# MLP up projections with weight tiles as the stationary operand, activations and their remainder side by side as the moving operand

## The chip, the cores and the metric

The program runs on one core of a Trainium2 chip. The metric is the device time of one execution in microseconds (us). The kernel before takes 2648.08 us, the median of three runs.

## The reference

Two transformer blocks in float32 on 256 tokens of 2048 features: a block with a pooling mixer and dilated attention, then one with a gated delta rule, a convolution and cross attention to a memory. Both end in the MLP that this change touches:

```python
h = rmsnorm(x, norm_mlp_g[l])
x = x + jnp.square(jax.nn.relu(h @ w_up[l])) @ w_down[l]      # w_up 2048 x 8192, w_down 8192 x 2048
```

The second block has the same with `mlp_w1_2`, `mlp_w2_2`.

## The kernel before, in words

Every large product is a sum of three: each float32 number is split into a high part and a remainder, both held as fp32r, and hi·hi, hi·remainder and remainder·hi are accumulated in PSUM. Weights come from HBM in *steps* of 1 MB (128 partitions x 2048 numbers); they are never reused.

- SyncE issues one DMA per step into one of five slots `weights_raw` (`load`), once the step five back is used up (`w_used`).
- ScalarE copies a step to `weights_hi` (three slots, L1249), two steps ahead of TensorE at most; VectorE writes the remainder `weights_lo` over the raw slot (L1691).
- TensorE multiplies (`step`, L677, L678, L681): a step holds two k-tiles of 128 rows by 1024 columns of weights. For each of two token tiles and two k-tiles a 128x128 tile of activations is stationary and 512 weight columns move: 24 matmuls of 128x512 a step. Eight steps are a *pass*: 1024 output columns, in one of two groups of four PSUM banks.

The activations stand transposed as `stationary_hi` and `stationary_lo` (features on partitions), which the steps read. They are made by TensorE transposes and a split on ScalarE and VectorE.

In `mlp` a half of the 8192 hidden features takes four up passes and then two down passes of 16 steps each; there are two halves and two MLPs, so 16 up passes and 8 down passes. An up pass leaves tokens on partitions, while the down passes want hidden features on partitions. So after each up pass ScalarE takes relu with the scale `rstd` (`relu`, L1300), VectorE multiplies by the positive part (`square`, L1743), TensorE turns the result with 16 transposes (`turn_hidden`, L729, placed two steps into the next pass), and ScalarE and VectorE split it into `hidden_hi` (L1307) and `hidden_lo` (L1751). For the MLP norm `rstd` holds one over the mean square, and the scale stands on the hidden rows once.

Each engine runs its instructions in program order. ScalarE and VectorE loop over steps k: `split_next(s0 + k)` splits step k+1, and after it comes what belongs to that point of the pass.

Of the kernel before, what the change touches and what calls it, by code (L numbers as in the profile page):

```python
# [7 lines left out]
F32 = mybir.dt.float32  # L8
F32R = mybir.dt.float32r
# [4 lines left out]
P = 128  # L14
# [14 lines left out]
AHEAD = 1  # L29

# [60 lines left out]
def build(nc, x, mem, vectors, squares, alibi, pool_avg, w_in, pool_w, pool_scale, w_out, w_up, w_down,  # L91
          final_g, w_in2, a_log, dt_bias, w_out2, wq, wk, wv, wo, w1, w2, final_g2, out):
    ctx = ExitStack()
    with ctx:
# [12 lines left out]
        HHI = at("stationary_hi", [P, KT, T], 16, F32R)  # L107
        HLO = at("stationary_lo", [P, KT, T], 32, F32R)
# [29 lines left out]
        JUNK = at("squares_unused", [P, TT, D], A0 + 64)  # L138
        AHI = at("hidden_hi", [P, HK, T], A0 + 0, F32R)
        ALO = at("hidden_lo", [P, HK, T], A0 + 32, F32R)  # L140
        R = at("hidden", [P, TT, COLS], A0 + 64)
# [140 lines left out]
        relu_done = sem("relu_done")  # L282
        r_turned = sem("r_turned")
# [122 lines left out]
        HALF_PASSES = 6  # L406
# [45 lines left out]
        def blocks(w):  # L452
            return w.rearrange("(s j p) n -> s p j n", j=STEP, p=P)
# [5 lines left out]
        def _(sp):  # L459
# [165 lines left out]
        def _(pe):  # L625
# [90 lines left out]

            def mlp(m, s_m, p_m, h, while_last=None):
                pe.wait_ge(ht_lo, KT * h + KT // 2)
                for half in range(2):
                    s0, p0, a0 = s_m + half * HALF_STEPS, p_m + half * HALF_PASSES, 32 * m + 16 * half  # L720
# [12 lines left out]
                    for p in range(4):  # L733
                        if p >= 2:

                            pe.wait_ge(at_hi, a0 + 4 * (p - 1))
                            pe.wait_ge(at_lo, a0 + 4 * (p - 1))
                        for k in range(PS):
                            if p >= 1 and k == 2:
                                turn_hidden(p - 1)  # L740
                            if p == 0 and half == 0:
                                if k == 2:

                                    left(p0 - 1)
                                    turn8(residual, 1, 1)
                                stationary(h, STEP * (k + 1))
                            step(s0 + p * PS + k, HHI, HLO, STEP * k, p0 + p, k == 0, k == PS - 1)
                    for d in range(2):
                        n = HK // STEP
                        pe.wait_ge(at_hi, a0 + 12 + 4 * d)  # L750
                        pe.wait_ge(at_lo, a0 + 12 + 4 * d)
                        for k in range(n):
                            if d == 0 and k == 2:
                                turn_hidden(3)
                            if d == 0 and k == 12:
                                pe.wait_ge(at_hi, a0 + 16)
                                pe.wait_ge(at_lo, a0 + 16)
                            if while_last and half and d and k == 4:
                                while_last()
                            step(s0 + 4 * PS + d * n + k, AHI, ALO, STEP * k, p0 + 4 + d, k == 0, k == n - 1)  # L760
# [477 lines left out]
        def _(act):  # L1238
# [47 lines left out]
            def mlp(m, s_m, p_m, norm, h, g_of):  # L1286
                for half in range(2):
                    s0, p0, r0 = s_m + half * HALF_STEPS, p_m + half * HALF_PASSES, 32 * m + 16 * half
# [983 lines left out]
```

## Time and profile before

| what | value |
|---|---|
| median, lowest, highest of three runs | 2648.08, 2645.53, 2648.35 us |
| span of the profiled execution, first to last instruction | 2644.1 us |
| TensorE: matmul busy, weight loads busy | 2623.9 us (99%), 2190.3 us (83%) |
| VectorE, ScalarE busy | 1448.3 us (55%), 1106.6 us (42%) |
| matmuls | 12420 |
| mean DMA rate | 178 GB/s |

The time of the profiled execution as a whole is not recorded apart from its span; the median of the runs is 4.0 us above that span. "Busy" of TensorE is not a rate: matmuls overlap in the records (a 128x512 one is shown with 390 ns), so how long each costs is read from the distance between starts, or from the chain of waits, which gives each its own share of the time.

### The profile page before, as it was taken

What the parts mean: (1) busy time and instruction counts of PE and PEld (TensorE: products, weight loads), DVE (VectorE), ACT (ScalarE), POOL (GpSimd) and SP (SyncE); (2) the same over time, 40 slices, a digit from 0 to 9 for tenths busy, and PEclk for the clock granted to TensorE, in tenths of its full rate; (3) what the DMA queues carried; (4) which work ended last, traced back from release to release, by engine and by line L of the source; (5) the groups of instructions that cost most, each with busy time, mean ns of one, the idle gap of its engine ahead of it and who ended that gap; (6) DMA issues with size and microseconds to landing.
All of it is one profiled execution on the core that took longest, in us unless ns stands there. A gap on an engine that the chain in (4) does not pass through costs nothing.

```text
span 2644.1 us, 28753 instructions
## 1 busy us (share of the span) xinstructions
PE 2623.9 (99%) x12420; PEld 2190.3 (83%) x12420; DVE 1448.3 (55%) x1249; ACT 1106.6 (42%) x966; POOL 40.7 (2%) x58
## 2 busy tenths in 40 slices
PE   9999999999999999999999999999999999999998
PEld 7888888888888888888888888887888888888887
DVE  5464545544455445677658796544554544455444
ACT  5344444433344334454225444443454433344433
POOL 0000000000000000001000000000000000000000
PEclk9999999999999999999999999999999999999999
DMA  8544655566555566655324355553555566555564
GB/s 292 198 147 143 206 185 185 187 191 191 193 189 184 186 188 190 233 181 161 111 82 142 121 187 185 176 160 127 175 207 177 190 191 191 192 190 181 187 194 138
DMA packets 121980, 471.56 MB, mean 178 GB/s; under 512 B 7328, under 2 KB 7968, under 8 KB 120704
## 3 DMA queue, kind: packets, MB, share of 16 engines
q1 hardware_dynamic: 119440, 456.62, 53.2%
q0 software_dynamic: 1856, 11.54, 1.2%
q8 instruction: 99, 1.62, 0.2%
q10 hardware_dynamic: 560, 1.57, 0.2%
q14 instruction: 25, 0.20, 0.0%
HBM read 465.51 MB, written 4.19 MB: 178 GB/s over the span
## 4 chain that ended last, share of the span: by engine, by line
PE 96%; DVE 3%; ACT 1%; issue 0%; DMA 0%; POOLq 0%; SPq 0%; POOL 0%; ACTq 0%; DVEq 0%
PE ps L677 29%; PE ps L678 29%; PE ps L681 29%; PE ps L913 2%; DVE conv_out L1903 1%; PE ps L729 1%; PE ps L641 1%; PE ps L799 1%; DVE weights_lo L1691 1%; PE ps L1165 1%; PE ps L1181 1%; PE ps L1085 0%; PE ps L1087 0%; PE ps L1010 0%; PE ps L880 0%; PE ps L871 0%
## 5 line engine op out<-in xcount | busy, mean ns | idle before, releaser
L1691 DVE TENSOR_TENSOR weights_lo<-weights_raw,weights_hi 128x2048 fp32r<-128x2048 f32 x431 | 987.6, 2292 | 958.6 <-ACT weights_hi L1249 958.6
L1249 ACT ACTIVATE weights_hi<-weights_raw 128x2048 fp32r<-128x2048 f32 x431 | 826.4, 1918 | 1165.4 <-PE ps L681 1164.1
L677 PE MATMUL ps<-weights_hi,stationary_hi 128*128 128x512 f32 x2432 | 960.2, 395 | 6.5 <-ACT stationary_hi L1592 2.5
L678 PE MATMUL ps<-weights_lo,stationary_hi 128*128 128x512 f32 x2432 | 949.9, 391 | 0.0
L681 PE MATMUL ps<-weights_hi,stationary_lo 128*128 128x512 f32 x2432 | 750.9, 390 | 0.0
L677 PEld LDWEIGHTS ps<-weights_hi,stationary_hi 128*128 128x128 f32 x2432 | 457.5, 188 | 103.1 <-issue 5.2
L681 PEld LDWEIGHTS ps<-weights_hi,stationary_lo 128*128 128x128 f32 x2432 | 457.7, 188 | 96.3
L678 PEld LDWEIGHTS ps<-weights_lo,stationary_hi 128*128 128x128 f32 x2432 | 458.2, 188 | 92.4 <-issue 0.7
L677 PE MATMUL ps<-weights_hi,hidden_hi 128*128 128x512 f32 x1016 | 396.0, 390 | 0.0
L678 PE MATMUL ps<-weights_lo,hidden_hi 128*128 128x512 f32 x1016 | 395.8, 390 | 0.0
L681 PE MATMUL ps<-weights_hi,hidden_lo 128*128 128x512 f32 x1016 | 312.9, 389 | 0.0
L677 PEld LDWEIGHTS ps<-weights_hi,hidden_hi 128*128 128x128 f32 x1016 | 190.8, 188 | 39.4
L681 PEld LDWEIGHTS ps<-weights_hi,hidden_lo 128*128 128x128 f32 x1016 | 190.8, 188 | 39.4
L678 PEld LDWEIGHTS ps<-weights_lo,hidden_hi 128*128 128x128 f32 x1016 | 190.9, 188 | 39.2
L1903 DVE SCALAR_TENSOR_TENSOR conv_out<-conv_in,vectors,conv_out 128x256 f32<-128x256 f32 x240 | 100.8, 500 | 0.2
L1267 ACT ACTIVATE stationary_hi<-ps,vectors 128x256 fp32r<-128x256 f32 x120 | 45.5, 488 | 50.7 <-PE ps L641 50.7
L1704 DVE SCALAR_TENSOR_TENSOR stationary_lo<-ps,vectors,stationary_hi 128x256 fp32r<-128x256 f32 x120 | 48.5, 477 | 21.7 <-ACT stationary_hi L1267 21.7
L1307 ACT ACTIVATE hidden_hi<-ps 128x512 fp32r<-128x512 f32 x64 | 33.1, 604 | 62.5 <-PE ps L729 62.5
L1751 DVE TENSOR_TENSOR hidden_lo<-ps,hidden_hi 128x512 fp32r<-128x512 f32 x64 | 39.8, 685 | 35.4 <-ACT hidden_hi L1307 35.4
L1300 ACT ACTIVATE hidden<-ps,rstd 128x1024 f32<-128x1024 f32 x32 | 35.7, 1117 | 37.6 <-PE ps L681 37.6
L1743 DVE SCALAR_TENSOR_TENSOR hidden<-ps,hidden 128x1024 f32<-128x1024 f32 x32 | 39.1, 1222 | 18.5 <-ACT hidden L1300 18.5
L1724 DVE TENSOR_TENSOR residual<-ps,residual 128x1024 f32<-128x1024 f32 x26 | 31.8, 1222 | 0.1
(312 smaller groups left out, 1011.0 us busy)
## 6 DMA issues: line engine op xcount, KB each, us to landing
weights_raw<-in_w SPq DMA_DIRECT2D x128, 1024.0 KB, 5.2
weights_raw<-in_w_in SPq DMA_DIRECT2D x79, 1024.0 KB, 5.1
weights_raw<-in_w_up SPq DMA_DIRECT2D x64, 1024.0 KB, 4.8
weights_raw<-in_w_down SPq DMA_DIRECT2D x64, 1024.0 KB, 5.5
weights_raw<-in_w_out SPq DMA_DIRECT2D x32, 1024.0 KB, 5.4
weights_raw<-in_wk SPq DMA_DIRECT2D x16, 1024.0 KB, 5.3
weights_raw<-in_wv SPq DMA_DIRECT2D x16, 1024.0 KB, 5.3
weights_raw<-in_wq SPq DMA_DIRECT2D x16, 1024.0 KB, 5.3
```

The source lines that it names most:

```text
L677: pe.matmul(o, xh, WHI[:, slot, j, c * BANK:(c + 1) * BANK], start=first and j == 0, stop=False)
L678: pe.matmul(o, xh, WLO[:, low, j, c * BANK:(c + 1) * BANK], start=False, stop=False)
L681: mm = pe.matmul(o, xl, WHI[:, slot, j, c * BANK:(c + 1) * BANK], start=False, stop=last and j == STEP - 1)
L913: last = pe.matmul(ps[:, 4 + u // 4, (u % 4) * P:(u % 4 + 1) * P], lhs[:, u, :], rhs[:, u, :], start=True, stop=True)
L1249: act.activation(WHI[:, s % NSPLIT], RAW[:, s % NRAW], ACT.Copy).then_inc(hi_ready, 1)
L1267: act.activation(HHI[:, k, :], v, ACT.Copy, scale=gain(g(k))).then_inc(ht_hi, 1)
L1300: act.activation(R[:, t, :], ps[:, g + 2 * t:g + 2 * t + 2, :].rearrange("p b n -> p (b n)"), ACT.Relu, scale=rstd_of(norm, t)).then_inc(r ...
L1691: dve.tensor_tensor(WLO[:, s % NRAW], RAW[:, s % NRAW], WHI[:, s % NSPLIT].bitcast(F32), ALU.subtract).then_inc(lo_ready, 1)
L1704: dve.scalar_tensor_tensor(HLO[:, k, :], v, gain(g(k)), HHI[:, k, :].bitcast(F32), ALU.mult, ALU.subtract).then_inc(ht_lo, 1)
L1743: dve.scalar_tensor_tensor(R[:, t, :], ps[:, g + 2 * t:g + 2 * t + 2, :].rearrange("p b n -> p (b n)"), 0.0, R[:, t, :], ALU.max, ALU.mult ...
L1751: dve.tensor_tensor(ALO[:, k:k + 2, :].rearrange("p k t -> p (k t)"), ps[:, g + b, :], AHI[:, k:k + 2, :].bitcast(F32).rearrange("p k t -> ...
L1903: last = dve.scalar_tensor_tensor(COUT31[:, c, :], src, dw_tap(j, c), COUT31[:, c, :], ALU.mult, ALU.add)
```

## The change

In the up passes a 128x128 tile of weights is stationary (128 of the columns of `w_up`) and the activations move. High part and remainder of a k-tile's activations now lie side by side (`HX`), so one matmul of 128x512 with the high weights gives both hi·hi (256 columns) and hi·remainder (the other 256), and one of 128x256 with the low weights adds remainder·hi to the first 256. The output has features on partitions and tokens on the free axis, as the down passes want it, and `turn_hidden` is gone. The two sums in a bank are added by ScalarE (copy of the second part) and VectorE (add, then relu times value). An up pass is 512 features in four steps of four k-tiles; there are 32 of them. `rstd` moves behind the down products (`add_scaled`, and the last additions). Rows of `w_up` are loaded in pieces of 512 columns rather than 1024.

```diff
+UPS = 4
+UPT = BANK // P
...
-        HHI = at("stationary_hi", [P, KT, T], 16, F32R)
-        HLO = at("stationary_lo", [P, KT, T], 32, F32R)
+        HX = at("stationary", [P, KT, 2, T], 16, F32R)
+        HHI, HLO = HX[:, :, 0, :], HX[:, :, 1, :]
...
-        R = at("hidden", [P, TT, COLS], A0 + 64)
+        UB = at("up_second_part", [P, UPT, T], A0 + 64)
+        UZ = at("up", [P, UPT, T], A0 + 68)
...
+            def load_up(s, src):
+                if s >= NRAW:
+                    sp.wait_ge(w_used, s - NRAW + 1)
+                dst = RAW[:, s % NRAW].rearrange("p j (h c) -> p (j h) c", c=BANK)
+                sp.dma_start(dst, src).then_inc(raw_landed[s % NRAW], 16)
...
-                    for p in range(4):
-                        c0 = half * HALF + p * COLS
-                        for k in range(PS):
-                            load(h0 + p * PS + k, blocks(up)[k, :, :, c0:c0 + COLS])
+                    for p in range(UP_PASSES):
+                        c0 = half * HALF + p * BANK
+                        for k in range(UPS):
+                            load_up(h0 + p * UPS + k, blocks(up, KT // UPS)[k, :, :, c0:c0 + BANK])
...
+            def up_tile(slot, low, q, c, k, group, start, stop):
+                col = (q % 2) * BANK + c * P
+                o = ps[:, 4 * group + c, :]
+                pe.matmul(o, WHI[:, slot, q // 2, col:col + P], HX[:, k, :, :].rearrange("p a t -> p (a t)"), start=start, stop=False)
+                return pe.matmul(o[:, 0:T], WLO[:, low, q // 2, col:col + P], HX[:, k, 0, :], start=False, stop=stop)
+
+            def up_step(s, k, p, arriving=None):
+
+                pe.wait_ge(hi_ready, s + 1)
+                pe.wait_ge(lo_ready, s + 1)
+                slot, low, group = s % NSPLIT, s % NRAW, GROUPS[p]
+                before = [n for n in range(p) if GROUPS[n] == group]
+                nq = KT // UPS
+                if k < UPS - 1:
+                    for q in range(nq):
+                        if arriving is not None:
+                            stationary(arriving, nq * k + q + 1)
+                        for c in range(UPT):
+                            if k == 0 and q == 0 and c % 2 == 0:
+                                pe.wait_ge((out0, out1)[c // 2], before[-1] + 1)
+                            mm = up_tile(slot, low, q, c, nq * k + q, group, k == 0 and q == 0, False)
+                else:
+                    for c in range(UPT):
+                        for q in range(nq):
+                            if arriving is not None and c == 0:
+                                stationary(arriving, nq * k + q + 1)
+                            mm = up_tile(slot, low, q, c, nq * k + q, group, False, q == nq - 1)
+                        if c == 1:
+                            mm.then_inc(t0_done, 1)
+                mm.then_inc(w_used, 1)
...
-                    def turn_hidden(p):
-                        pe.wait_ge(out0, p0 + p + 1)
-                        pe.wait_ge(out1, p0 + p + 1)
-                        g = 4 * (p % 2)
-                        for b in range(4):
-                            for k in range(2 * b, 2 * b + 2):
-                                for t in range(TT):
-                                    last = pe.transpose(ps[:, g + b, (k % 2) * T + t * P:(k % 2) * T + (t + 1) * P],
-                                                        R[:, t, k * P:(k + 1) * P], IDENT)
-                            last.then_inc(r_turned, 1)
...
+                    for p in range(UP_PASSES):
+                        for k in range(UPS):
+                            if (half, p, k) == (0, 0, 1):
+
+                                left(p0 - 1)
+                                turn8(residual, 1, 1)
+                            up_step(s0 + p * UPS + k, k, p0 + p, h if (half, p) == (0, 0) else None)
...
-                    def relu(p):
-                        act.wait_ge(rstd_ready, norm + 1)
-                        if p >= 1:
-                            act.wait_ge(r_turned, r0 + 4 * p)
-                        g = 4 * (p % 2)
-                        for t in range(TT):
-                            if t == 0:
+                    s0, p0 = s_m + half * HALF_STEPS, p_m + half * HALF_PASSES
+                    a0 = 2 * UP_PASSES * m + UP_PASSES * half
+
+                    def second_part(p):
+                        g = 4 * GROUPS[p0 + p]
+                        for n in range(2):
+                            if n == 0:
                                 act.wait_ge(t0_done, p0 + p + 1)
                             else:
-                                act.wait_ge(w_used, s0 + (p + 1) * PS)
-                            act.activation(R[:, t, :], ps[:, g + 2 * t:g + 2 * t + 2, :].rearrange("p b n -> p (b n)"), ACT.Relu,
-                                           scale=rstd_of(norm, t)).then_inc(relu_done, 1)
+                                act.wait_ge(w_used, s0 + (p + 1) * UPS)
+                            if p >= 1:
+                                act.wait_ge((out0, out1)[n], p0 + p)
+                            act.activation(UB[:, 2 * n:2 * n + 2, :], ps[:, g + 2 * n:g + 2 * n + 2, T:2 * T], ACT.Copy).then_inc(up_moved, 1)
 
                     def hidden_hi(p):
-                        g = 4 * (p % 2)
-                        for b in range(4):
-                            act.wait_ge(r_turned, r0 + 4 * p + b + 1)
-                            act.activation(AHI[:, 8 * p + 2 * b:8 * p + 2 * b + 2, :].rearrange("p k t -> p (k t)"), ps[:, g + b, :], ACT.Copy).then_inc(at_hi, 1)
+                        act.wait_ge(up_squared, a0 + p + 1)
+                        act.activation(AHI[:, UPT * p:UPT * p + UPT, :], UZ[:], ACT.Copy).then_inc(at_hi, 1)
...
+            def add_scaled(s_end, p, c0, norm):
...
+                    dve.scalar_tensor_tensor(v, ps[:, g:g + 2, :].rearrange("p b n -> p (b n)"), rstd_of(norm, t), v, ALU.mult, ALU.add).then_inc(o, 1)
...
-                    def square(p):
-                        g = 4 * (p % 2)
-                        for t, o in enumerate((out0, out1)):
-                            dve.wait_ge(relu_done, h0 + 2 * p + t + 1)
-                            dve.scalar_tensor_tensor(R[:, t, :], ps[:, g + 2 * t:g + 2 * t + 2, :].rearrange("p b n -> p (b n)"), 0.0, R[:, t, :],
-                                                     ALU.max, ALU.mult).then_inc(o, 1)
+                    s0, p0 = s_m + half * HALF_STEPS, p_m + half * HALF_PASSES
+                    a0 = 2 * UP_PASSES * m + UP_PASSES * half
+
+                    def squared(p):
+                        g = 4 * GROUPS[p0 + p]
+                        for n, o in enumerate((out0, out1)):
+                            dve.wait_ge(up_moved, 2 * (a0 + p) + n + 1)
+                            dve.tensor_tensor(UZ[:, 2 * n:2 * n + 2, :], ps[:, g + 2 * n:g + 2 * n + 2, 0:T], UB[:, 2 * n:2 * n + 2, :], ALU.add).then_inc(o, 1)
+                        dve.wait_ge(out1, p0 + p + 1)
+                        dve.scalar_tensor_tensor(UZ[:], UZ[:], 0.0, UZ[:], ALU.max, ALU.mult).then_inc(up_squared, 1)
 
                     def hidden_lo(p):
-                        g = 4 * (p % 2)
-                        for b in range(4):
-                            dve.wait_ge(at_hi, a0 + 4 * p + b + 1)
-                            k = 8 * p + 2 * b
-                            dve.tensor_tensor(ALO[:, k:k + 2, :].rearrange("p k t -> p (k t)"), ps[:, g + b, :],
-                                              AHI[:, k:k + 2, :].bitcast(F32).rearrange("p k t -> p (k t)"), ALU.subtract).then_inc(at_lo, 1)
+                        dve.wait_ge(at_hi, a0 + p + 1)
+                        dve.tensor_tensor(ALO[:, UPT * p:UPT * p + UPT, :], UZ[:], AHI[:, UPT * p:UPT * p + UPT, :].bitcast(F32), ALU.subtract).then_inc(at_lo, 1)
...
```

How TensorE's order changes. Before, at the third step of the second up pass of the first MLP: the end of a step, then the transposes of the pass before (`squares` is the identity, `hidden` the squared relu).

```order
L681 MATMUL ps<-weights_hi,stationary_lo 128x512 x2
L729 MATMUL ps<-squares,hidden 128x128 [waits out1,out0]
L729 MATMUL ps<-squares,hidden 128x128 x15
L677 MATMUL ps<-weights_hi,stationary_hi 128x512 [waits lo_ready,hi_ready]
L678 MATMUL ps<-weights_lo,stationary_hi 128x512
```

Of the changed kernel, where the third up pass of the first MLP begins; `stationary` is now the moving operand and `weights_hi`, `weights_lo` are the stationary one:

```order
L731 MATMUL ps<-stationary,weights_hi 128x512
L732 MATMUL ps<-stationary,weights_lo 128x256
L731 MATMUL ps<-stationary,weights_hi 128x512 [waits out0,lo_ready,hi_ready]
L732 MATMUL ps<-stationary,weights_lo 128x256
L731 MATMUL ps<-stationary,weights_hi 128x512
L732 MATMUL ps<-stationary,weights_lo 128x256
L731 MATMUL ps<-stationary,weights_hi 128x512 [waits out1]
```

A step is now 16 pairs of a 128x512 and a 128x256 matmul, with a new weight tile for each of the two, and no transposes stand between steps.

ScalarE before, at the end of the first up pass (`t0_done`: first half of the pass's last step, `w_used`: the step's end):

```order
L1249 ACTIVATE weights_hi<-weights_raw 128x2048 [waits w_used,raw_landed2]
L1300 ACTIVATE hidden<-ps,rstd 128x1024 [waits t0_done,rstd_ready]
L1300 ACTIVATE hidden<-ps,rstd 128x1024 [waits w_used]
L1249 ACTIVATE weights_hi<-weights_raw 128x2048 [waits w_used,raw_landed3]
L1249 ACTIVATE weights_hi<-weights_raw 128x2048 [waits w_used,raw_landed4]
L1307 ACTIVATE hidden_hi<-ps 128x512 [waits r_turned] x4
```

and of the changed kernel:

```order
L1270 ACTIVATE weights_hi<-weights_raw 128x2048 [waits w_used,raw_landed3]
L1321 ACTIVATE up_second_part<-ps 128x512 [waits t0_done]
L1321 ACTIVATE up_second_part<-ps 128x512 [waits w_used]
L1270 ACTIVATE weights_hi<-weights_raw 128x2048 [waits w_used,raw_landed4]
L1325 ACTIVATE hidden_hi<-up 128x1024 [waits up_squared]
```

The split of the hidden features follows one step after the pass's end rather than two, and comes after every fourth step, not every eighth.

## Rows read from the trace of the kernel before

**Rows 1.** The page: the chain that ended last, by engine and by line.
```profile
PE 96%; DVE 3%; ACT 1%; issue 0%; DMA 0%; POOLq 0%; SPq 0%; POOL 0%; ACTq 0%; DVEq 0%
```
**Rows 2.** Windows: up passes, then down passes; us, busy (instructions), PEclk, DMA share, GB/s.
```profile
314.00:495.60 181.60, 181.60 (x836) 151.36 (x835) 93.33 (x60) 81.69 (x64) 1.49 (x3) 1.00 0.56 191
495.50:680.00 184.50, 184.50 (x824) 153.07 (x823) 85.73 (x43) 67.68 (x39) 0.00 (x0) 1.00 0.61 193
```
**Rows 3.** The chain in order of time, up passes: start us, us, what.
```profile
355.92 0.45 PE ps L681 x2
...
361.36 0.45 PE ps L681 x2
...
369.98 1.75 PE ps L729 x16
...
415.29 1.75 PE ps L729 x16
```
**Rows 4.** The chain from the beta and alpha product (L926 to L928) on.
```profile
1062.36 0.12 PE ps L926
...
1067.98 0.23 PE ps L677
```
**Rows 5.** Timeline, loads alone, same place: start us, us, engine, line, what.
```profile
1062.20 0.10 PEld L927 LDWEIGHTS ps<-stationary_hi,w_ba_lo 128*16 128x16 f32 x1
1062.32 0.09 PEld L928 LDWEIGHTS ps<-stationary_lo,w_ba_hi 128*16 128x16 f32 x1
```
**Rows 6.** Timeline at L1110 (matmuls of two columns): matmuls, then loads.
```profile
1621.44 3.63 PE L1110 MATMUL ps<-squares,conv_squares 128*128 128x2 f32 x32
```
```profile
1621.21 3.77 PEld L1110 LDWEIGHTS ps<-squares,conv_squares 128*128 128x128 f32 x32
```
**Rows 7.** Groups by form: weight loads, count, busy us, mean ns of one.
```profile
L678 PEld LDWEIGHTS ps<-weights_lo,stationary_hi 128*128 128x128 f32 x2432 | 458.2, 188 | 92.4 <-issue 0.7
L913 PEld LDWEIGHTS ps<-inverse_t,level_product 128*128 128x128 f32 x160 | 18.5, 192 | 0.5
```
**Rows 8.** The chain: matmuls of 128x128 and of 128x256 in plain float32.
```profile
1289.56 3.57 PE ps L913 x32
...
1771.16 6.91 PE ps L1165 x32
```
**Rows 9.** Timeline of loads and matmuls in an up pass.
```profile
345.33 0.19 PEld L678 LDWEIGHTS ps<-weights_lo,stationary_hi 128*128 128x128 f32 x1
345.56 0.19 PEld L677 LDWEIGHTS ps<-weights_hi,stationary_hi 128*128 128x128 f32 x1
```
```profile
345.33 0.39 PE L677 MATMUL ps<-weights_hi,stationary_hi 128*128 128x512 f32 x1
345.55 0.39 PE L678 MATMUL ps<-weights_lo,stationary_hi 128*128 128x512 f32 x1
```
**Rows 10.** The page's groups, ScalarE and VectorE: busy us, mean ns of one.
```profile
L1307 ACT ACTIVATE hidden_hi<-ps 128x512 fp32r<-128x512 f32 x64 | 33.1, 604 | 62.5 <-PE ps L729 62.5
L1751 DVE TENSOR_TENSOR hidden_lo<-ps,hidden_hi 128x512 fp32r<-128x512 f32 x64 | 39.8, 685 | 35.4 <-ACT hidden_hi L1307 35.4
L1300 ACT ACTIVATE hidden<-ps,rstd 128x1024 f32<-128x1024 f32 x32 | 35.7, 1117 | 37.6 <-PE ps L681 37.6
L1743 DVE SCALAR_TENSOR_TENSOR hidden<-ps,hidden 128x1024 f32<-128x1024 f32 x32 | 39.1, 1222 | 18.5 <-ACT hidden L1300 18.5
L1724 DVE TENSOR_TENSOR residual<-ps,residual 128x1024 f32<-128x1024 f32 x26 | 31.8, 1222 | 0.1
```
**Rows 11.** Timeline of ScalarE at a pass's end: in brackets the idle time before.
```profile
359.13 1.12 ACT L1300 ACTIVATE hidden<-ps,rstd 128x1024 f32<-128x1024 f32 x1 [1.54 <-PE ps L681]
360.14 1.91 ACT L1249 ACTIVATE weights_hi<-weights_raw 128x2048 fp32r<-128x2048 f32 x1
364.63 1.92 ACT L1249 ACTIVATE weights_hi<-weights_raw 128x2048 fp32r<-128x2048 f32 x1 [2.58 <-PE ps L681]
```
**Rows 12.** DMA queues in 0 to 30 us, then in 314 to 495 us: packets, MB, share of 16 engines.
```profile
q10 hardware_dynamic: 272, 0.52, 5.4%
```
```profile
q1 hardware_dynamic: 8704, 33.56, 54.9%
...
weights_raw<-in_w_up SPq DMA_DIRECT2D x28, 1024.0 KB, 4.8
```

More of the change, by code:

```diff
@@ L281, in build @@
         ht_lo = sem("ht_lo")
[L282 to L283 removed]
+        up_moved = sem("up_moved")
+        up_squared = sem("up_squared")
         at_hi = sem("at_hi")
@@ L733, in mlp @@
[L733 to L747, printed above, removed]
+                    s0, p0, a0 = s_m + half * HALF_STEPS, p_m + half * HALF_PASSES, 2 * UP_PASSES * m + UP_PASSES * half
@@ L752, in mlp @@
                         for k in range(n):
[L753 to L757, printed above, removed]
+                            if d == 0 and k == n - 2:
+                                pe.wait_ge(at_hi, a0 + UP_PASSES)
+                                pe.wait_ge(at_lo, a0 + UP_PASSES)
@@ L758, in mlp @@
                             if while_last and half and d and k == 4:
                                 while_last()
-                            step(s0 + 4 * PS + d * n + k, AHI, ALO, STEP * k, p0 + 4 + d, k == 0, k == n - 1)
+                            step(s0 + UP_PASSES * UPS + d * n + k, AHI, ALO, STEP * k, p0 + UP_PASSES + d, k == 0, k == n - 1)
             def keep_busy(n):
@@ L1309, in mlp @@
                     for k in range(AHEAD, HALF_STEPS + AHEAD):
                         split_next(s0 + k)
-                        p = k // PS - 1
-                        if 0 <= p < 4 and k % PS == 0:
-                            relu(p)
-                        elif 0 <= p < 4 and k % PS == 2:
-                            hidden_hi(p)
+                        if UPS <= k < UPS * (UP_PASSES + 1) and k % UPS == 0:
+                            second_part(k // UPS - 1)
+                        elif UPS <= k < UPS * (UP_PASSES + 1) and k % UPS == 1:
+                            hidden_hi(k // UPS - 1)
@@ L1316, in mlp @@
                         elif half == 0 and k == 1:
+                            split_turned(h, lambda k: g_of + k, 1, 1)
+                        elif half == 0 and k == 3:
                             act.wait_ge(out1, p_m)
-                            squares_of(X, norm)
-                        elif half == 0 and k == 2:
-                            split_turned(h, lambda k: g_of + k, 1, 1)
+                            squares_of(X, norm, MLP_JUNK)
                         elif m == 0 and half == 1 and k == HALF_STEPS - HK // STEP + 4:
@@ L1728, in ahead @@
                     split_next(s0 + k)
+            def add_scaled(s_end, p, c0, norm):
+                dve.wait_ge(rstd_ready, norm + 1)
+                for t, o in enumerate((out0, out1)):
+                    if t == 0:
+                        dve.wait_ge(t0_done, p + 1)
+                    else:
+                        dve.wait_ge(w_used, s_end)
+                    g = 4 * GROUPS[p] + 2 * t
+                    v = X[:, t, c0:c0 + COLS]
+                    dve.scalar_tensor_tensor(v, ps[:, g:g + 2, :].rearrange("p b n -> p (b n)"), rstd_of(norm, t), v, ALU.mult, ALU.add).then_inc(o, 1)
             def ahead_and_residual(s_next, p):
@@ L1754, in mlp @@
+                    def hidden_lo(p):
+                        dve.wait_ge(at_hi, a0 + p + 1)
+                        dve.tensor_tensor(ALO[:, UPT * p:UPT * p + UPT, :], UZ[:], AHI[:, UPT * p:UPT * p + UPT, :].bitcast(F32), ALU.subtract).then_inc(at_lo, 1)
                     for k in range(AHEAD, HALF_STEPS + AHEAD):
                         split_next(s0 + k)
-                        p = k // PS - 1
-                        if 0 <= p < 4 and k % PS == 0:
-                            square(p)
-                        elif 0 <= p < 4 and k % PS == 2:
-                            hidden_lo(p)
-                        elif half == 0 and k == 2:
+                        if UPS <= k < UPS * (UP_PASSES + 1) and k % UPS == 0:
+                            squared(k // UPS - 1)
+                        elif UPS <= k < UPS * (UP_PASSES + 1) and k % UPS == 1:
+                            hidden_lo(k // UPS - 1)
+                        elif half == 0 and k == 1:
@@ L1762, in mlp @@
                             split_turned(h, lambda k: g_of + k, 1, 1)
                         elif k == HALF_STEPS // 2 + HK // STEP:
-                            add_residual(s0 + k, p0 + 4, 0)
+                            add_scaled(s0 + k, p0 + UP_PASSES, 0, norm)
                         elif m == 0 and half == 1 and k == HALF_STEPS - HK // STEP + 4:
@@ L1772, in mlp @@
                         elif k == HALF_STEPS and (m, half) != (1, 1):
-                            add_residual(s0 + k, p0 + 5, COLS)
+                            add_scaled(s0 + k, p0 + UP_PASSES + 1, COLS, norm)
             dve.memset(ZEROS[:], 0.0).then_inc(zeros_ready, 1)
```

26 lines of the change are left out of this document (13 added, 13 removed).

## The prediction

> **What bounds the kernel now.** First the chain of waits: 96% of the span runs through TensorE [rows 1]. Then the windows of one half of an MLP: in its up passes TensorE is busy for all of 181.60 us, while VectorE has 93 us of work, ScalarE 82 and the DMA engines a share of 0.56, at the full granted clock [rows 2]. Nothing waits there that could be shortened; only TensorE's own instructions count. Their durations must not be read from the groups (390 ns for a 128x512 matmul), since they overlap. In the chain the same place of a step recurs after 5.44 us (355.92 to 361.36) [rows 3]; a step has 24 matmuls, so one costs 226.7 ns. The 16 transposes after an up pass stand in the chain with 1.75 us [rows 3], 109 ns each. Pass to pass is 415.29 - 369.98 = 45.31 us, which is 8 x 5.44 + 1.75 = 45.27: the up stage is these two terms and nothing else.
>
> **What goes.** 16 up passes with 16 transposes each: 16 x 1.75 = 28.0 us. The matmuls: 16 passes x 8 steps x 24 = 3072 at 226.7 ns, 696.4 us. Together 724.4 us.
>
> **What comes.** 32 passes x 4 steps x 16 = 2048 pairs: a 128x512 matmul and a 128x256 one. The columns that move are the same as before (3072 x 512 = 2048 x 768), but there are 4096 matmuls for 3072, each with a weight tile of its own, and half of them are short. So the case is decided by what a short fp32r matmul costs when the next 128x128 tile has to be loaded under it.
>
> The long one: 226.7 ns, unchanged; its successor's load begins as it begins (the load for L678 at 345.33, where the matmul of L677 starts; the next at 345.56 beside 345.55 [rows 9]) and has time enough.
>
> The short one: the trace has 48 fp32r matmuls of 256 columns in a row, 1062.36 to 1067.98 us in the chain [rows 4], which is 117.1 ns each. But their weight tiles have only 16 columns (0.09 us a load [rows 5]); with 128 columns this pairing doesn't occur. What a load of 128 columns costs when nothing covers it shows where matmuls have two columns: 32 loads take 3.77 us, so (3.77 - 0.19)/31 = 115 ns with one delay among them, and 32 matmuls in 3.63 us, (3.63 - 0.25)/31 = 109 [rows 6]. Matmuls of 128 columns in plain float32 with new weights each come to 3.57/32 = 112 ns [rows 8]. So a load needs 109 to 115 ns, though its record says 188 or 192 [rows 7]; the records overlap, as the spacing of 112 at a duration of 192 shows. Those loads are of plain float32; the fp32r ones have the same record (188), and I take the same spacing. The load of 109 to 115 just fits under a matmul of 117.1. Bounds for the short one: from below 109 (the load alone); from above 188, the whole record of a load laid bare, and beyond it 6.91/32 = 216 ns, the 128x256 matmul in plain float32 [rows 8], another type of operand. I take 118, next to the row of the same type and length, with 1 ns for a load that is as good as tight.
>
> The up stage after: 2048 x (226.7 + 118) ns = 705.9 us. Against 724.4 that is -18.5 us: the matmuls cost 9.5 us more, the transposes give 28.0 back. Each nanosecond of the short matmul is 2.05 us of the sum, and the gain is gone at 118 + 18.5/2.05 = 127 ns.
>
> A rule of the Trainium skill speaks against this. "TensorE: Matmul & The Clock Gate", section "Packing small matmuls", says that a load of weights runs beside matmuls in flight only where it goes to other rows of the array. Here all loads fill all rows and yet run beside [rows 9], so the trace disagrees. By the rule the 1024 additional pairs would lay bare a load each, by the 112 ns of the rows 115 us, and the change would end near 2744 us.
>
> **What is hidden.** ScalarE and VectorE. With E the end of an up pass on TensorE: ScalarE copies the second half of the second part (128x512 from PSUM, 604 ns by L1307), VectorE adds it (685 by L1751) and multiplies (128x1024, 1222 by L1743) [rows 10]; done near E + 2.7. Then ScalarE has put the split of the step after next in between (1.9 us), and writes `hidden_hi` (1117 by L1300), done near E + 3.9; VectorE follows with the low weights (2.29 us, from about E + 2.8) and then `hidden_lo` (1222), done near E + 6.4. Behind these waiting instructions the splits of weights are queued, for which TensorE waits. But the split after the pass's end is for the step that starts at E + 11: before too ScalarE splits it right behind its work for the pass (360.14) and the next one only when TensorE is a step further (364.63, after 2.58 us idle) [rows 11]. There are some 5 us in hand. By pass of 22 us VectorE has 4 x 2.29 + 2 x 0.685 + 2 x 1.222 = 13.0 us and ScalarE 4 x 1.92 + 2 x 0.604 + 1.117 = 10.0. The hidden features of pass 7 are wanted 14 steps later, and the bank group of a pass a whole pass later. Zero from both; if the cover failed, each pass start would show it, 32 times.
>
> `add_scaled` in place of the plain addition: both forms take 1222 ns from PSUM [rows 10], and the last two pairs of additions, which are on the chain, change alike: zero. The transposes of the residual at the start of each MLP move one step forward; two of these, and the steps behind them need the result one and a half steps later: zero. Ends of both signs within 1 us.
>
> The loads: rows of 2 KB in place of 4 KB for `w_up`, 512 packets a step. In the up passes a packet of 4 KB takes 0.549 x 16 x 181 us / 8704 = 183 ns; the queue that brought a part of x in pieces of 2 KB took 0.054 x 16 x 30 us / 272 = 95 ns a packet [rows 12]. So a step needs 512 x 95/16 = 3.0 us of all engines against 256 x 183/16 = 2.9, in 5.5 us. SyncE's queue may issue a step's load two steps before ScalarE wants it, 11 us against 4.8 to landing [rows 12]. Zero; a packet of 2 KB would have to cost 172 ns before it decides.
>
> **Sum.** Span 2644.1 - 18.5 = 2625.6 us; the median of the runs is 4.0 above this span, so 2629.6 us.
>
> **The rivals.**
> 1. *The short matmul doesn't cover its load* (the side of slower). Place: each of the 2048 second loads and swaps. For it: the records of 188 ns, loads at 83% of the span, and that the pairing isn't in the trace; also that a 128x512 fp32r matmul already costs 13 ns more than 512 columns at 2.4 GHz (213.3), and I don't know from what. Against it: the rows at 109 to 115. It decides from 127 ns: at 135 it is +16 us (2664), at 188 it is 2048 x 70 ns = 143 us over the forecast (2773), at 216 it is 2830. Chance 0.11, the milder half of it likelier.
> 2. *A new wait at pass boundaries*: ScalarE's and VectorE's tail, 0.3 us at each of 32 starts gives back 10 us: 2640. For it: twice as many boundaries; against it: 5 us in hand. Chance 0.05.
> 3. *The loads in 2 KB rows decide*: if a packet of 2 KB cost as much as one of 4 KB (183 ns), a step would take 5.86 us and 128 steps 44 us more: 2673. Against it 95 ns. Chance 0.02.
> 4. *A larger gain*: the load alone sets the short matmul, 109 ns: another 18 us, 2611. For it: half of 226.7 is 113. Against it the 48 at 117.1. Chance 0.07. The Trainium skill, same page, section "Back-to-back issue gap", gives N/2.4 + 2.5 ns, 109 for 256 columns; by that the sum would also be 2611, but it gives 216 for 512 columns, where the rows have 226.7.
> 5. The forecast, short matmul 115 to 122: 0.75; by itself 2623 to 2638.
>
> **Range and chances.** Rivals 2 and 4 in large part and the first edge of rival 1 belong in the range: 2618 to 2646. What can be told from no change here is about 0.2%, 5.3 us, so faster means under 2642.8: the forecast, rivals 4 and 2 (most) and a little of 1, 0.86. Within 0.2% (to 2653, short matmul 124 to 130): 0.06. Slower 0.08.
>
> **What would show it.** In the chain of the up passes: L731 with 0.23 and L732 with 0.12 us, a step of 5.52 us, a pass of 22.1, no L729, a half's up stage at 176.5 us. Matmuls 12420 - 3072 - 256 + 4096 = 13188. ScalarE's and VectorE's splits still preceded by idle time that TensorE ends. Wrong if L732 stands at 0.13 or more, if the starts of steps have idle time on TensorE released by `weights_lo` or a DMA, or if the distance of a 128x512 matmul changes from 226.7 ns when activations move and weights stand.

## The result, and the profile after

The changed kernel takes 2639.67 us, the median of 11 runs (2638.12 to 2641.41), the kernel before 2647.82 (11 runs). The ratio is 0.9976, 95% interval [0.9967, 0.9984]: a gain of 0.24%, or 6.4 us. The two medians are 8.2 us apart, and the span of the profiled execution fell by 6.0, from 2644.1 to 2638.1 us. By any of the three the gain is a third to under a half of the 18.5 us forecast.

The page after, busy time and instructions, then the chain by engine (against [rows 1]):

```profile
PE 2617.4 (99%) x13188; PEld 2211.5 (84%) x13188; DVE 1485.3 (56%) x1281; ACT 1110.3 (42%) x966; POOL 40.6 (2%) x58
...
PE 96%; DVE 3%; ACT 1%; issue 0%; DMA 0%; POOLq 0%; SPq 0%; POOL 0%; ACTq 0%; DVEq 0%
```

13188 matmuls as counted; still TensorE alone. Windows over the up passes of a first half and of the second half behind it; columns as in [rows 2]:

```profile
314.80:493.00 178.20, 178.20 (x1035) 155.95 (x1034) 102.85 (x70) 83.56 (x66) 1.49 (x3) 1.00 0.61 194
668.90:849.50 180.60, 180.60 (x1024) 156.69 (x1023) 99.75 (x62) 76.76 (x55) 0.00 (x0) 1.00 0.58 187
```

The windows do not end exactly with the stages, which the starts of the matmuls give: 314.81 to 494.15 us is 179.3 us for the first half's 8 x 64 pairs with 16 transposes of the residual (1.75 us) among them, 668.25 to 849.14 is 180.9 us for the second half's with none. Before, the first half's columns and four sets of 16 transposes (three of the hidden rows, one of the residual) took 181.6. TensorE is busy throughout, at the full granted clock. So the difference between the two halves is neither waits nor clock, but the matmuls themselves: their distance must be read. Timeline of TensorE in a first half, then in a second (start us, us, engine, line):

```profile
345.08 0.39 PE L731 MATMUL ps<-stationary,weights_hi 128*128 128x512 f32 x1
345.31 0.27 PE L732 MATMUL ps<-stationary,weights_lo 128*128 128x256 f32 x1
345.42 0.40 PE L731 MATMUL ps<-stationary,weights_hi 128*128 128x512 f32 x1
345.65 0.28 PE L732 MATMUL ps<-stationary,weights_lo 128*128 128x256 f32 x1
...
346.12 0.40 PE L731 MATMUL ps<-stationary,weights_hi 128*128 128x512 f32 x1
```

```profile
669.30 0.40 PE L731 MATMUL ps<-stationary,weights_hi 128*128 128x512 f32 x1
...
670.00 0.40 PE L731 MATMUL ps<-stationary,weights_hi 128*128 128x512 f32 x1
670.24 0.28 PE L732 MATMUL ps<-stationary,weights_lo 128*128 128x256 f32 x1
670.36 0.40 PE L731 MATMUL ps<-stationary,weights_hi 128*128 128x512 f32 x1
```

Three pairs take 346.12 - 345.08 = 1.04 us in the first half and 670.36 - 669.30 = 1.06 us in the second. A pass has 346.7 ns a pair in the first halves of both MLPs and 353.3 in the second halves (distance of the long matmuls' starts, mean over a pass). The forecast had 344.7. Read to the nanosecond, the distances repeat without change. I call such a repeating pattern a *raster*, and there are three:

| raster | where | long to long, ns | long to short, short to long (means) |
|---|---|---|---|
| A | first half of the first MLP | 343, 350 in turn: 346.7 | 231.7, 115.0 |
| B | first half of the second MLP | 346 or 347 always: 346.7 | 230.0, 116.7 |
| C | both second halves | 349, 350, 361 in turn: 353.3 | 236.7, 116.7 |

So the distance behind the long matmul is 3 to 10 ns above its 226.7 in all of them, and the one behind the short matmul is at or below the 118 of the forecast. The weight loads, in the same stretch as the first fence:

```profile
345.31 0.19 PEld L731 LDWEIGHTS ps<-stationary,weights_hi 128*128 128x128 f32 x1
345.43 0.19 PEld L732 LDWEIGHTS ps<-stationary,weights_lo 128*128 128x128 f32 x1
```

Each still begins with the matmul ahead of it, as in [rows 9], the one under the short matmul too: it is covered.

The other engines at a pass's end (339.0 us; ScalarE, then VectorE; idle time before in brackets), against [rows 11]:

```profile
339.53 1.91 ACT L1270 ACTIVATE weights_hi<-weights_raw 128x2048 fp32r<-128x2048 f32 x1
341.65 1.06 ACT L1325 ACTIVATE hidden_hi<-up 128x1024 fp32r<-128x1024 f32 x1 [0.21 <-DVE up L1774]
344.64 1.92 ACT L1270 ACTIVATE weights_hi<-weights_raw 128x2048 fp32r<-128x2048 f32 x1 [1.93 <-PE ps L732]
```

```profile
339.67 0.69 DVE L1772 TENSOR_TENSOR up<-ps,up_second_part 128x512 f32<-128x512 f32 x1 [1.23 <-ACT up_second_part L1321]
340.40 1.23 DVE L1774 SCALAR_TENSOR_TENSOR up<-up 128x1024 f32<-128x1024 f32 x1
341.54 2.29 DVE L1708 TENSOR_TENSOR weights_lo<-weights_raw,weights_hi 128x2048 fp32r<-128x2048 f32 x1
343.74 1.22 DVE L1778 TENSOR_TENSOR hidden_lo<-up,hidden_hi 128x1024 fp32r<-128x1024 f32 x1
```

`hidden_lo` ends at 345.0, 6 us after the pass; the next split still finds ScalarE idle until TensorE frees a slot. As forecast. The loads of `w_up` take 5.2 us to land instead of 4.8, and nobody waits for them:

```profile
weights_raw<-in_w_up SPq DMA_DIRECT2D x64, 1024.0 KB, 5.2
```

TensorE's waits differ in one place, the first up step of the second MLP: L731 waits 0.18 us at its first matmul and 0.20 at its third for the addition of the residual, where L677 before waited 0.2 once. The third bank is now wanted two pairs after the first rather than half a step later.

### The profile page after: what moved, and what is told of

It reads as the page before. It is cut to its first block, busy times and chain, and to the rows that moved or that the text cites. A ratio compares the mean times of both kernels' runs of the same rounds, so it can differ in the third digit from the quotient of the medians.

```text
span 2638.1 us, 30356 instructions
## 1 busy us (share of the span) xinstructions
PE 2617.4 (99%) x13188; PEld 2211.5 (84%) x13188; DVE 1485.3 (56%) x1281; ACT 1110.3 (42%) x966; POOL 40.6 (2%) x58
## 4 chain that ended last, share of the span: by engine, by line
PE 96%; DVE 3%; ACT 1%; issue 0%; DMA 0%; POOLq 0%; SPq 0%; POOL 0%; ACTq 0%; DVEq 0%
PE ps L688 20%; PE ps L692 20%; PE ps L689 20%; PE ps L731 18%; PE ps L732 9%; PE ps L934 2%; DVE conv_out L1928 1%; PE ps L652 1%; PE ps L820 1%; DVE weights_lo L1708 1%; PE ps L1186 1%; PE ps L1202 1%; PE ps L1106 0%; PE ps L1108 0%; PE ps L1031 0%; PE ps L901 0%
## 5 line engine op out<-in xcount | busy, mean ns | idle before, releaser
L731 PE MATMUL ps<-stationary,weights_hi 128*128 128x512 f32 x2048 | 717.6, 396 | 0.4 <-DVE residual L1741 0.4
L732 PE MATMUL ps<-stationary,weights_lo 128*128 128x256 f32 x2048 | 572.9, 280 | 0.0
L688 PE MATMUL ps<-weights_hi,stationary 128*128 128x512 f32 x1408 | 559.4, 397 | 6.2 <-ACT stationary L1609 2.5
L689 PE MATMUL ps<-weights_lo,stationary 128*128 128x512 f32 x1408 | 549.5, 390 | 0.0
L731 PEld LDWEIGHTS ps<-stationary,weights_hi 128*128 128x128 f32 x2048 | 384.2, 188 | 92.2 <-issue 0.6
L692 PE MATMUL ps<-weights_hi,stationary 128*128 128x512 f32 x1408 | 435.3, 390 | 0.0
L732 PEld LDWEIGHTS ps<-stationary,weights_lo 128*128 128x128 f32 x2048 | 386.3, 189 | 0.1
L688 PEld LDWEIGHTS ps<-weights_hi,stationary 128*128 128x128 f32 x1408 | 265.2, 188 | 63.5 <-issue 4.5
L692 PEld LDWEIGHTS ps<-weights_hi,stationary 128*128 128x128 f32 x1408 | 264.9, 188 | 56.2
L689 PEld LDWEIGHTS ps<-weights_lo,stationary 128*128 128x128 f32 x1408 | 265.3, 188 | 53.4 <-issue 0.7
L1288 ACT ACTIVATE stationary<-ps,vectors 128x256 fp32r<-128x256 f32 x120 | 45.6, 489 | 54.4 <-PE ps L652 54.4
L1772 DVE TENSOR_TENSOR up<-ps,up_second_part 128x512 f32<-128x512 f32 x64 | 44.0, 688 | 42.4 <-ACT up_second_part L1321 42.4
```

The source lines that it names most:

```text
L688: pe.matmul(o, xh, WHI[:, slot, j, c * BANK:(c + 1) * BANK], start=first and j == 0, stop=False)
L689: pe.matmul(o, xh, WLO[:, low, j, c * BANK:(c + 1) * BANK], start=False, stop=False)
L692: mm = pe.matmul(o, xl, WHI[:, slot, j, c * BANK:(c + 1) * BANK], start=False, stop=last and j == STEP - 1)
L731: pe.matmul(o, WHI[:, slot, q // 2, col:col + P], HX[:, k, :, :].rearrange("p a t -> p (a t)"), start=start, stop=False)
L732: return pe.matmul(o[:, 0:T], WLO[:, low, q // 2, col:col + P], HX[:, k, 0, :], start=False, stop=stop)
L1288: act.activation(HHI[:, k, :], v, ACT.Copy, scale=gain(g(k))).then_inc(ht_hi, 1)
```

## The experiments

**Which term is off?** Four kernels, measured together.

First the transposes alone, in the kernel before:

```diff
                                 for t in range(TT):
-                                    last = pe.transpose(ps[:, g + b, (k % 2) * T + t * P:(k % 2) * T + (t + 1) * P],
-                                                        R[:, t, k * P:(k + 1) * P], IDENT)
+                                    if (k % 2, t) == (0, 0):
+                                        last = pe.transpose(ps[:, g + b, (k % 2) * T + t * P:(k % 2) * T + (t + 1) * P],
+                                                            R[:, t, k * P:(k + 1) * P], IDENT)
```

> The kernel before with 4 instead of 16 transposes after each up pass (one for each bank; three quarters of the hidden features are left unturned, so the sums are not the reference's). Theory A (the transposes stand on TensorE's path with their full 109 ns): 16 x 12 x 109.4 ns = 21.0 us less, 2627 us. Theory B (something else would be late without them, so removing them gives less): 5 to 15 us less, and idle time of TensorE at L677 behind L729.

Measured 2626.08 us (5 runs), ratio to before 0.9922 [0.9909, 0.9934]; the span falls by 20.2 us to 2623.9. The chain at such a place, against the 1.75 us of [rows 3]:

```profile
370.64 0.44 PE ps L730 x4
```

Theory A came true: twelve transposes are worth what the chain gives them. The term of 28.0 us stands, and the missing gain is in the matmuls.

Then the second matmul of each pair on all 512 columns:

```diff
-                return pe.matmul(o[:, 0:T], WLO[:, low, q // 2, col:col + P], HX[:, k, 0, :], start=False, stop=stop)
+                return pe.matmul(o, WLO[:, low, q // 2, col:col + P], HX[:, k, :, :].rearrange("p a t -> p (a t)"), start=False, stop=stop)
```

> The changed kernel with the second matmul of a pair on all 512 columns too (it adds low weights times remainder, a fourth product that the kernel leaves away). No matmul is short then. Theory A (only the mix of lengths costs extra): a pair is 2 x 226.7 = 453.3 ns, against 350.4 now, +103 ns x 2048 = +211 us, 2851 us. Theory B (a 128x512 matmul with weights standing costs 234 by itself): 468 ns, +241 us, 2880 us.

Measured 2851.74 us (4 runs), ratio 1.0773 [1.0756, 1.0789]. Its chain, where three pairs (L731 to L731) take 1.36 us, 453 ns each:

```profile
399.86 0.23 PE ps L731
...
401.22 0.23 PE ps L731
```

Theory A came true. Weights that stand, activations that move and a new tile for each matmul cost nothing: at equal lengths a 128x512 one has its 226.7 ns. The extra comes only when short ones stand among them.

Next, is it the alternation?

```diff
...
-                            mm = up_tile(slot, low, q, c, nq * k + q, group, k == 0 and q == 0, False)
+                            up_long(slot, q, c, nq * k + q, group, k == 0 and q == 0)
+                        for c in range(UPT):
+                            mm = up_short(low, q, c, nq * k + q, group, False)
...
+                            up_long(slot, q, c, nq * k + q, group, False)
+                        for q in range(nq):
+                            mm = up_short(low, q, c, nq * k + q, group, q == nq - 1)
...
```

> The changed kernel with the order inside a step changed: four 128x512 matmuls in a row, then the four 128x256 ones that belong to them, instead of alternating. Theory A (alternating lengths cost the extra 7 to 13 ns a pair, as the long one is 226.7 ns wherever it stands among its like): a pair falls to 226.7 plus 113 to 117, that is 340 to 344 ns, 13 to 21 us less, 2619 to 2627 us. Theory B (the extra belongs to weights that stand while activations move, or to each load): pairs stay at 347 to 353 and the time within 2 us of the changed kernel.

Measured 2640.67 us (11 runs), ratio 0.9977 [0.9969, 0.9986]: the same as the changed kernel. Timeline, four long (L730) and four short ones (L734):

```profile
401.05 1.09 PE L730 MATMUL ps<-stationary,weights_hi 128*128 128x512 f32 x4
401.98 0.64 PE L734 MATMUL ps<-stationary,weights_lo 128*128 128x256 f32 x4
402.46 1.09 PE L730 MATMUL ps<-stationary,weights_hi 128*128 128x512 f32 x4
```

Eight matmuls in 1.41 us; a pair costs 350.8 ns, and here it does so in first and second halves alike. With 1024 pairs at 346.7 and 1024 at 353.3 the changed kernel has a mean of 350.0, so the equal time is partly a coincidence: the grouped order has one speed of its own between the two. My Theory A for this run has fallen: with a quarter of the changes of length the extra has not become smaller. Theory B's number came true, but its reason is excluded by the run before.

Last, is it what ran just ahead?

```diff
+                            if (half, p, k) == (1, 0, 0):
+                                earlier = [n for n in range(p0) if GROUPS[n] == GROUPS[p0]]
+                                pe.wait_ge(out0, earlier[-1] + 1)
+                                for _ in range(1):
+                                    pe.transpose(ps[:, 4 * GROUPS[p0], 0:P], IDENT, IDENT)
                             up_step(s0 + p * UPS + k, k, p0 + p, h if (half, p) == (0, 0) else None)
```

> The changed kernel with one plain float32 transpose (128x128, of the identity, result overwritten) in front of the up passes of the second half of each MLP; two such places in all. In the trace of the changed kernel the pair of matmuls takes 346.7 ns in the first half of each MLP and 353.3 ns in the second, and the first step of the first half, ahead of the 16 transposes, has 353.3 too. Theory A (the raster into which TensorE falls is set by what runs just ahead of the stream): the second halves go to 346.7, 1024 pairs x 6.7 ns = 6.8 us less, about 2633 us beside 2639.7. Theory B (the second half differs by its weights, slots or contents): nothing changes but +0.2 us.

Measured 2633.31 us (5 runs, 2632.43 to 2634.72), ratio 0.9949 [0.9937, 0.9962]. That is 6.4 us under the changed kernel, for two added transposes. The timeline behind one (L773), in the second half:

```profile
668.17 0.27 PE L773 MATMUL ps<-squares 128*128 128x128 f32 x1
668.20 0.47 PE L731 MATMUL ps<-stationary,weights_hi 128*128 128x512 f32 x1
...
668.63 0.40 PE L731 MATMUL ps<-stationary,weights_hi 128*128 128x512 f32 x1
...
669.67 0.39 PE L731 MATMUL ps<-stationary,weights_hi 128*128 128x512 f32 x1
```

Three pairs in 669.67 - 668.63 = 1.04 us, and so for all 512 pairs up to the down passes: 346.7 ns (raster A). Theory A came true. This kernel is the fastest of the case.

**What sets the raster, and what is the base?** Two kernels with another choice in each of the 32 up passes, each executed once with its trace; read are the starts of the long matmuls over a pass's last three steps.

```diff
+                if k == 0:
+                    kind, size = NUDGES[UP_ORDER.index(p)]
+                    if kind:
+                        pe.wait_ge(out0, before[-1] + 1)
+                    if kind == "turn":
+                        for _ in range(size):
+                            pe.transpose(ps[:, 4 * group, 0:P], IDENT, IDENT)
+                    elif kind == "short":
+                        pe.matmul(ps[:, 4 * group, 0:size], WHI[:, slot, 0, 0:P], HX[:, 0, :, :].rearrange("p a t -> p (a t)")[:, 0:size], start=True, stop=True)
```

> The changed kernel with something else at the start of each of the 32 up passes, results overwritten: nothing, one to four plain float32 transposes, or one fp32r matmul of 16 to 512 columns. Read is the mean time of a pair in each pass. Theory A (any shift of the stream sets the raster anew): passes jump between 346.7 and 353.3 ns, and perhaps 340, with fp32r matmuls too. Theory B (only a change to plain float32 and back sets it): passes after transposes have 346.7, passes after an fp32r matmul or nothing keep what the pass before had. Time: within 12 us of 2636.

Only two values came, 346.7 and 353.3 ns a pair (340 never). In the order in which the passes run, with what was added ahead of each (a bare number is the columns of one fp32r matmul):

| half of an MLP | 346.7 ns a pair | 353.3 ns a pair |
|---|---|---|
| first MLP, first half | nothing; 16; 32; 48; 64 | then 96; 128; 160 |
| first MLP, second half | 1, 2 and 3 transposes (passes 2 to 4) | nothing (pass 1); 192; 4 transposes; 224; 256 |
| second MLP, first half | nothing; 320; 384; 480 (passes 1, 3, 5, 8) | 288; 352; 416; 448 (passes 2, 4, 6, 7) |
| second MLP, second half | one transpose; one transpose; 256 (passes 3, 5, 6) | 512; nothing; 128; one transpose; 32 (passes 1, 2, 4, 7, 8) |

Here is a pass behind 320 columns, three pairs in 1.04 us:

```profile
1979.71 0.39 PE L734 MATMUL ps<-stationary,weights_hi 128*128 128x512 f32 x1
...
1980.75 0.39 PE L734 MATMUL ps<-stationary,weights_hi 128*128 128x512 f32 x1
```

and the next, behind 352 columns, in 1.06 us:

```profile
1999.77 0.40 PE L734 MATMUL ps<-stationary,weights_hi 128*128 128x512 f32 x1
...
2000.83 0.40 PE L734 MATMUL ps<-stationary,weights_hi 128*128 128x512 f32 x1
```

Theory A came true but for the 340: fp32r matmuls set it as well as transposes do. The same one doesn't always set the same value: one transpose gave 346.7 three times and 353.3 once, 256 columns gave both. The raster before would explain this: one transpose behind raster C gave A all three times and behind B it gave C; 256 columns behind C kept C and behind A gave B. It can't be the whole story. In the first pass, where nothing was added, the 16 transposes of the residual follow on a first step in raster C here as in the changed kernel; this execution went on in B, that of the changed kernel in A.

```diff
+                moving = HX[:, k, :, :].rearrange("p a t -> p (a t)")
+                pe.matmul(o[:, 0:lengths[0]], WHI[:, slot, q // 2, col:col + P], moving[:, 0:lengths[0]], start=start, stop=False)
+                return pe.matmul(o[:, 0:lengths[1]], WLO[:, low, q // 2, col:col + P], moving[:, 0:lengths[1]], start=False, stop=stop)
```

> The changed kernel with other column counts (N1, N2) of the two matmuls of a pair, one choice for each up pass; columns are left out or added, so the hidden features are not the reference's. Theory A (each fp32r matmul costs its columns at 2.4 GHz plus a fixed 13.3 ns): (256,256) 240 ns, (384,384) 347, (448,448) 400, (512,256) 347, (512,384) 400, (512,512) 453; (512,128) is held up by the load, 227 + 109 to 115. Theory B (6.25% on the columns, nothing fixed): (256,256) 227 ns, (384,384) 340, (448,448) 397, (512,256) 340, (512,384) 397, with something extra from changing lengths only, so that equal lengths have none. Time: not told by this run, 2640 +- 100 us.

| columns of a pair | columns at 2.4 GHz + 2 x 13.3 | measured, ns a pair |
|---|---|---|
| 256, 256 (two passes) | 240.0 | 240.0, 240.0 |
| 384, 384 | 346.7 | 346.7 |
| 320, 256; 384, 256; 448, 256 | 266.7; 293.3; 320.0 | 266.7; 293.3; 320.0 |
| 320, 320; 512, 240 | 293.3; 340.0 | 293.3; 340.0 |
| 512, 256 (six passes) | 346.7 | 346.7 to 348.4 in three, 353.4 in three |
| 416, 416; 448, 448 | 373.3; 400.0 | 376.6; 413.3 |
| 512, 384; 512, 448 | 400.0; 426.7 | 413.3 (both passes); 437.8 |
| 480, 480; 496, 496; 512, 512 | 426.7; 440.0; 453.3 | 433.3; 446.7; 453.3 |
| 512, 272; 512, 288; 512, 320 | 353.3; 360.0; 373.3 | 360.0; 363.3; 380.0 |
| 512, 352; 512, 416; 512, 480 | 386.7; 413.3; 440.0 | 393.3; 421.7; 446.7 |
| 288, 288 | 266.7 | 263.3 |
| 512, 192; 512, 224 | 320.0; 333.3 | 344.5; 343.4 |
| 512, 128 | 293.3 | 340.0 |

The chain of a pass with (256, 256) and of the one with (512, 128):

```profile
2032.98 0.12 PE ps L735
2033.10 0.12 PE ps L736
2033.22 0.12 PE ps L735
```

```profile
340.60 0.28 PE ps L735
340.94 0.28 PE ps L735
```

The loads beside that last chain:

```profile
340.72 0.19 PEld L735 LDWEIGHTS ps<-stationary,weights_hi 128*128 128x128 f32 x1
340.82 0.19 PEld L736 LDWEIGHTS ps<-stationary,weights_lo 128*128 128x128 f32 x1
```

Theory A came true for the base: in eight pairs of lengths, and in (512, 256) where it is fast, an fp32r matmul costs its columns at 2.4 GHz and 13.3 ns, so 120.0 ns for 256 columns. Theory B's 227 for (256, 256) is excluded. On the other pairs with 256 columns or more 3 to 13 ns come on top, which neither theory had, and (288, 288) lay 3.4 ns below its 266.7, so the 13.3 is no floor. (512, 128) is held by the load: the load for the short matmul starts 109 ns behind the load for the long one (340.72 and 340.82 rounded), and so 0.05 us after the long matmul instead of with it. 340.0 - 226.7 leaves 113.3 ns for 128 columns of weights. Whether the load also holds (512, 192) and (512, 224), which cost more than (512, 240) with its 340.0, was not looked into.

**The counter-test.** One small matmul that should spoil the good halves:

```diff
+                            if (half, p, k) == (0, 1, 0):
...
+                                pe.matmul(ps[:, 4 * g, 0:96], WHI[:, s % NSPLIT, 0, 0:P], HX[:, 0, 0, 0:96], start=True, stop=True)
```

> The changed kernel with one fp32r matmul of 96 columns (result overwritten) in front of the second up pass of the first half of each MLP, the only halves that run at 346.7 ns a pair; in the run with other starts such a matmul was followed by 353.3. Theory A (the raster is set by any shift ahead of the stream, and it alone decides the gain): 2 x 7 x 64 pairs x 6.7 ns = 6.0 us more than the changed kernel, 2645 to 2646 us, ratio to the kernel before 0.9995 to 1.000. Theory B (only transposes set it, the first halves are fast for another reason): no change, 2639.8 us.

Measured 2643.05 us (11 runs), ratio 0.9987 [0.9978, 0.9996]: 3.4 us more than the changed kernel, half of what Theory A had. The trace says why. Three pairs behind the added matmul in the first MLP, then in the second:

```profile
338.86 0.40 PE L731 MATMUL ps<-stationary,weights_hi 128*128 128x512 f32 x1
...
339.92 0.40 PE L731 MATMUL ps<-stationary,weights_hi 128*128 128x512 f32 x1
```

```profile
1948.84 0.39 PE L731 MATMUL ps<-stationary,weights_hi 128*128 128x512 f32 x1
...
1949.88 0.40 PE L731 MATMUL ps<-stationary,weights_hi 128*128 128x512 f32 x1
```

In the first MLP all seven passes behind the matmul went from 346.7 to 353.3, 448 pairs, 3.0 us; in the second MLP they stayed at 346.7. The time rose where the trace shows the slow raster, and only there. Which shift gives it I could not forecast, but the trace shows what differed: ahead of the same matmul of 96 columns stood raster A in the first MLP, which became C, and raster B in the second, which became A. In the run with other starts 96 columns behind A gave C too. The eleven runs of this kernel spread from 2641.02 to 2647.16 us, those of the changed kernel from 2638.12 to 2641.41, and only one of the eleven was traced. That in others both MLPs or neither were spoiled would fit the spread, but no trace shows it.

## Why the prediction was wrong

- *What bounds the kernel, the transposes (28.0 us), the counts*: right. 12 of 16 transposes gave back 20 to 21 us in the kernel before.
- *The long one: 226.7 ns, unchanged.* This step failed. It was read in a stream of 512-column matmuls alone. Among short ones the next start comes 230.0 to 236.7 ns later, which is the prediction's own last sign of being wrong, and the pair costs 346.7 or 353.3 ns, depending on the raster into which the stream falls. The second halves (1024 pairs) run at 353.3, which is 6.8 us. Adding one transpose ahead of each of them took 6.4 us off.
- *The short one: 118 ns*, taken from 48 matmuls at 117.1: mis-sized by 2.0 ns, 4.1 us. Those 48 have weight tiles of 16 columns; with full tiles pairs of (256, 256) cost 240.0 ns, so one is 120.0. That the width of the tile makes the difference was not tested. The distances would put all of the surplus on the long matmul (231.7 and 115.0); the split into 226.7 and 120.0 is the one that equal lengths give, and either way a pair has 346.7 for 344.7. The sum with 120 is -14.4 us, still within the range; with 6.8 us more it is -7.6. From the first up matmul of the first MLP to the last matmul of the kernel the traces have 313.64 to 2634.69 us before and 314.81 to 2628.56 after, which is 7.3 us less. The span shows 6.0 because the first MLP starts 1.2 us later, ahead of all up passes; in the traces of the changed kernel and its variants that start lies between 313.31 and 314.81, so most of it is what executions vary by.
- *The median, 4.0 us above the span*: mis-sized too. Each run for which both are recorded lies some 1.8 us above its own span, and the changed kernel's median 1.6 above the profiled 2638.1. The other 2 us would mean that the profiled execution of the kernel before was one of its faster ones.
- *Rival 1* had the right side but the wrong mechanism: the load (113.3 ns by the pair of 512 and 128 columns) is covered. Its remark that a 512-column matmul costs 13 ns more than its columns "and I don't know from what" was the place to look: a cost for each matmul, and there are a third more of them in the up passes.
- *What is hidden*: right for ScalarE, VectorE, `add_scaled` and the loads, but I wrote "zero" for bank waits and they came to 0.4 us at one place. *The Trainium skill's rule on loads and rows of the array*, which the prediction cites, was rightly set aside: all loads run beside the matmuls, and the 115 us that it would cost did not come.
- The direction was right; the size of the gain was off by a factor of two to three.

Not settled: why the stream of mixed lengths has rasters (they repeat after one, two or three pairs), and by what rule the work ahead picks one. That the work ahead picks it is shown; that the raster before takes part is suggested by the two runs, but was not tested by itself, and the same instructions led to A in one execution and to B in another. The mechanism is open.

## What to carry to other kernels

When the same columns are cut into more matmuls, each new matmul has a price of its own even where its weight load is covered (13.3 ns here): count matmuls as well as columns, and take the fixed part from rows of the same operand type and tile width. A duration read in a uniform stream holds for that stream; when a change mixes lengths, put a few ns a matmul into the range, and compare the same code in different places of the trace, since a difference there (346.7 against 353.3) shows what can still be won.

## What was not expected of the hardware

- A stream of 128x512 and 128x256 fp32r matmuls that alternate has two stable speeds, 346.7 and 353.3 ns a pair at the same granted clock of 1.00. It keeps one over hundreds of pairs and through pass boundaries until something else runs on TensorE; one transpose, which delays the stream by 0.12 us, was worth 3.4 us behind it (512 pairs, 6.7 ns each). In groups of four and four the same matmuls have a single speed, 350.8.
- 240 columns in place of 256 beside 512 gave 340.0 ns a pair, just the base of columns and 2 x 13.3, and 272 gave 360.0, 6.7 above it: only some lengths fit without loss. Fewer columns can even cost more: 224 beside 512 gave 343.4, 192 gave 344.5.
